# First and output products of the experts in one block, with bf16 gate products

## The chip, the cores and the metric

One core of one Trainium2 chip. TensorE multiplies matrices into PSUM, VectorE, ScalarE and GpSimd work on tiles in SBUF, and SyncE issues most of the DMA. The metric is the time of one execution in device microseconds (us); less is better.

## The reference

A decoder block on 1024 tokens of width 1024. The change lies in its last part, the product-key expert mixer. For each token eight heads choose 16 of 16384 experts each; every expert is a pair of vectors u and v. Cut to what matters:

```python
q = (xt @ wq).reshape(TOKEN_BLOCK, PEER_HEADS, 2, half)
s1 = jnp.einsum('thd,hkd->thk', q[:, :, 0], key1)
s2 = jnp.einsum('thd,hkd->thk', q[:, :, 1], key2)
v1, i1 = lax.top_k(s1, PEER_TOPK)
v2, i2 = lax.top_k(s2, PEER_TOPK)
...
sc, pos = lax.top_k(comb, PEER_TOPK)
...
gate = jax.nn.softmax(sc, axis=-1)
act = jax.nn.gelu(jnp.einsum('thkd,td->thk', u[experts], xt), approximate=False) * gate
return jnp.einsum('thk,thkd->td', act, v[experts])
```

After it come a residual, scaled by g2, and a final RMS norm.

## The kernel before

The kernel doesn't gather. It computes the hidden value of every expert for every token, multiplies it by a gate that is zero for experts not chosen, and multiplies the result by all of v. Each product of fp32 matrices is split: a = hi + lo, and three products (hi hi, hi lo, lo hi) in the fast fp32r format are added (`PARTS`). The two stages that the change touches come last, each a block of instruction streams that are written out by hand per engine and tied by semaphores.

**Stage `ph` (`stage_peer_topk`).** 136 tiles of weights pass through `tile` (L2121): 48 matmuls of 512 columns each. 8 tiles are the heads' query weights, 128 are u. Per tile SyncE loads `u_raw` (L2057), ScalarE makes the high part (`high`, L2175), VectorE the low part (`low`, L2254), ScalarE applies Gelu to the product (`take_hidden`, L2180) and SyncE stores it to DRAM (`hidden`, L2061). Two buffers of each alternate, so VectorE's low part for tile n + 2 is made after tile n has been taken. The stage has three parts:
- eight periods of `PERIOD` = 8 tiles, one per head. In each, VectorE does the top-k selection of one head between the splits (sixteen maxima and searches per round, pair sums, look-ups of 128x3200 elements),
- a bridge of 7 tiles, and transposes of the chosen expert numbers and shares,
- 64 gate steps of one tile and 16 tokens. For each token VectorE makes two operands: `row_hot`, one where the first half of the expert number matches (L2404), and `col_hot`, the share where the second half matches (L2408). Their fp32 product summed over the 128 picks (L2166) is the gate of all 16384 experts for that token. Four banks of four tokens alternate. ScalarE copies the banks out (L2245), and every fourth step SyncE stores 4 MB of gates (L2101).

All buffers of the stage are then given back and all engines meet at a barrier.

**Stage `px` (`stage_peer_mix`).** 32 turns of four groups of 128 experts. Per group SyncE loads v, the hidden values and the gates (L2469 to L2473, 0.5 MB each); VectorE multiplies hidden by gate (L2546), ScalarE makes high parts (L2522, L2524), VectorE low parts (L2548, L2550). A turn is 16 blocks of 12 matmuls of 512 columns (L2506) into 8 PSUM banks, and VectorE adds each block to an accumulator in SBUF (`held_tiles`, L2585). The operands of a turn are prepared during the turn before, at blocks 1, 5, 9 and 13. The accumulator is cleared first (L2554). In the last turn VectorE and ScalarE add the residual and normalise (L2563 to L2576), after a last load of g2, the norm weight and h.

## Time and profile before

| | |
|---|---|
| median of 3 runs | 5376.34 us (5373.24 to 5382.1) |
| profiled execution, its own time | 5366.34 us |
| its span | 5364.7 us |
| TensorE / VectorE / ScalarE / GpSimd busy | 94% / 53% / 29% / 5% |
| stage `ph` / stage `px`, first to last matmul | 2155.7 to 3901.3 / 3950.9 to 5346.6 us |
| mean DMA rate | 132 GB/s |

The busy share is an average over stages with different limits. Matmuls are pipelined: a matmul of 512 columns is shown as 389 ns long while the next starts after some 227 ns, so the price of one is read from starts, not from lengths. An fp32 product appears as two records.

### The profile page before, as it was taken

How to read it: one execution, taken by the hardware profiler on the slowest of the kernel's cores; microseconds unless marked ns; L12 is line 12 of the kernel's file. 1: busy time of each engine (PE TensorE's matmuls, PEld its weight loads, DVE VectorE, ACT ScalarE, POOL GpSimd, SP SyncE). 2: the span in 40 equal slices, each digit the busy share in tenths (PEclk: the TensorE clock that was granted, in tenths of full speed). 3: DMA queues.
4: the chain of work that ended last, by engine and by line, in shares of the span. 5: the costliest groups of instructions: out<-in, count | busy, mean ns of one | idle time of the engine just before them, and what ended most of it. 6: DMA issues, size and time to landing. Idle time of an engine off the chain costs nothing. (4 is left out here: it accounts for less than half of the span.)

```text
span 5364.7 us, 69919 instructions
## 1 busy us (share of the span) xinstructions
PE 5029.8 (94%) x25070; PEld 4136.0 (77%) x25070; DVE 2869.8 (53%) x6216; ACT 1572.6 (29%) x2427; POOL 254.4 (5%) x340
## 2 busy tenths in 40 slices
PE   5599979998997998999999999999969999999998
PEld 1388867776886777788888888888858888888887
DVE  6511027776566344466666455555545555555556
ACT  2211125565565332222222222222211111111111
POOL 1100000000333110000000000000000000000000
PEclk8798989999998999999999999999989999999999
DMA  7332123332554552222222243333365555555554
GB/s 292 114 118 89 65 84 122 127 126 102 189 184 144 181 165 75 89 85 91 87 91 95 110 161 140 137 153 144 129 175 142 145 147 142 144 148 142 143 147 132
DMA packets 479906, 710.29 MB, mean 132 GB/s; under 512 B 286432, under 2 KB 334960, under 8 KB 474472
## 3 DMA queue, kind: packets, MB, share of 16 engines
q1 hardware_dynamic: 451080, 598.51, 34.9%
q0 software_dynamic: 22880, 96.79, 5.3%
q10 hardware_dynamic: 5760, 12.59, 0.6%
q8 instruction: 107, 1.75, 0.1%
q14 instruction: 79, 0.65, 0.0%
HBM read 487.32 MB, written 220.49 MB: 132 GB/s over the span
## 5 line engine op out<-in xcount | busy, mean ns | idle before, releaser
L2121 PE MATMUL ph_hid_ps<-ph_n_hi,ph_u_hi 128*128 128x512 f32 x2176 | 855.0, 393 | 8.1 <-ACTq L2196 8.0
L2121 PE MATMUL ph_hid_ps<-ph_n_lo,ph_u_hi 128*128 128x512 f32 x2176 | 847.9, 390 | 0.0
L2121 PE MATMUL ph_hid_ps<-ph_n_hi,ph_u_lo 128*128 128x512 f32 x2176 | 847.8, 390 | 0.0
L2506 PE MATMUL px_out_ps<-px_v_hi,px_weight_hi 128*128 128x512 f32 x2048 | 798.0, 390 | 49.6 <-DVEq L2557 49.6
L2506 PE MATMUL px_out_ps<-px_v_lo,px_weight_hi 128*128 128x512 f32 x2048 | 797.7, 390 | 0.0
L2506 PE MATMUL px_out_ps<-px_v_hi,px_weight_lo 128*128 128x512 f32 x2048 | 797.6, 389 | 0.0
L2585 DVE TENSOR_TENSOR held_tiles<-held_tiles,px_out_ps 128x512 f32<-128x512 f32 x512 | 350.4, 685 | 594.2 <-PE px_out_ps L2506 594.2
L2254 DVE TENSOR_TENSOR ph_u_lo<-ph_u_raw,ph_u_hi 128x1024 fp32r<-128x1024 f32 x136 | 166.7, 1226 | 707.4 <-ACT ph_u_hi L2175 707.0
L2180 ACT ACTIVATE ph_hidden<-ph_hid_ps 128x1024 f32<-128x1024 f32 x128 | 131.2, 1025 | 1209.7 <-PE ph_hid_ps L2121 1209.7
L2506 PEld LDWEIGHTS px_out_ps<-px_v_hi,px_weight_hi 128*128 128x128 f32 x2048 | 385.0, 188 | 129.9 <-DVEq L2557 49.8
L2121 PEld LDWEIGHTS ph_hid_ps<-ph_n_hi,ph_u_hi 128*128 128x128 f32 x2176 | 409.4, 188 | 91.9 <-DVE ph_u_lo L2254 8.3
L2121 PEld LDWEIGHTS ph_hid_ps<-ph_n_hi,ph_u_lo 128*128 128x128 f32 x2176 | 409.0, 188 | 85.3
L2121 PEld LDWEIGHTS ph_hid_ps<-ph_n_lo,ph_u_hi 128*128 128x128 f32 x2176 | 409.4, 188 | 82.8
L2506 PEld LDWEIGHTS px_out_ps<-px_v_hi,px_weight_lo 128*128 128x128 f32 x2048 | 385.0, 188 | 80.2
L2506 PEld LDWEIGHTS px_out_ps<-px_v_lo,px_weight_hi 128*128 128x128 f32 x2048 | 385.1, 188 | 79.9
L2524 ACT ACTIVATE px_weight_hi<-px_raw 128x1024 fp32r<-128x1024 f32 x128 | 136.1, 1064 | 1040.9 <-DVE px_raw L2546 1040.9
L2408 DVE TENSOR_SCALAR held_tiles<-ph_iota,held_tiles 128x128 f32<-128x128 f32 x1024 | 284.3, 341 | 0.0
L2166 PEld LDWEIGHTS ph_gate_ps<-held_tiles,ph_row_hot 128*128 128x128 f32 x2048 | 238.4, 192 | 5.0
L859 PE MATMUL at_acc<-proj_n1T_hi,at_w_hi 128*128 128x512 f32 x512 | 213.8, 418 | 30.0 <-ACTq L1050 27.1
L2166 PE MATMUL ph_gate_ps<-held_tiles,ph_row_hot 128*128 128x128 f32 x2048 | 238.8, 275 | 0.0
L859 PE MATMUL at_acc<-proj_n1T_hi,at_w_lo 128*128 128x512 f32 x512 | 203.7, 398 | 0.0
L859 PE MATMUL at_acc<-proj_n1T_lo,at_w_hi 128*128 128x512 f32 x512 | 203.0, 396 | 0.0
(319 smaller groups left out, 7926.2 us busy)
## 6 DMA issues: line engine op xcount, KB each, us to landing
ph_u_raw<-in_tiles SPq DMA_DIRECT2D x136, 512.0 KB, 3.6
scratch_hidden<-ph_hidden SPq DMA_DIRECT2D x128, 512.0 KB, 2.6
scratch_gate_tiles<-ph_gates SPq DMA_DIRECT2D x16, 4096.0 KB, 12.8
px_v_raw<-in_v_experts SPq DMA_DIRECT2D x128, 512.0 KB, 3.5
px_raw<-scratch_hidden SPq DMA_DIRECT2D x128, 512.0 KB, 5.3
px_gate<-scratch_gate_tiles SPq DMA_DIRECT2D x128, 512.0 KB, 6.5
proj_w_ch<-in_w_ch SPq DMA_DIRECT2D x49, 512.0 KB, 3.7
mr_w<-in_ada_w POOLq DMA_DIRECT2D x6, 4096.0 KB, 19.6
```

The lines of the kernel that those rows point to most:

```text
L859: mm = pe.matmul(acc[c][:], w[p][a][:, k, :], n1T[b][:, k, c * HALF:(c + 1) * HALF], start=(k == 0 and a + b == 0), stop=(k == KD - 1 and ...
L2121: mm = pe.matmul(hid_ps[r][:, c * HALF:(c + 1) * HALF], u[r][a][:, k, :], n2[b][:, k, c * HALF:(c + 1) * HALF], start=(k == 0 and a + b == ...
L2166: mm = pe.matmul(gate_ps[b][:, t, :], row_hot[b][:, t, :], col_hot[b][:, t, :], start=True, stop=True)
L2180: act.activation(hidden[r][:], hid_ps[r][:], ACT.Gelu).then_inc(taken[r], 1)
L2254: dve.tensor_tensor(u[r][1][:], u_raw[r][:], u[r][0][:].bitcast(F32), ALU.subtract).then_inc(u_lo[r], 1)
L2408: ins = dve.tensor_scalar(col_hot[b][:, t, :], iota[:], chosenT[:, 1, tok], chosenT[:, 2, tok], ALU.is_equal, ALU.mult)
L2506: mm = pe.matmul(out_ps[b][:], weight[q][j][wp][:, t * P:(t + 1) * P], v[q][j][vp][:, c * HALF:(c + 1) * HALF], start=(j == 0 and wp + vp ...
L2524: act.activation(weight[q][j][0][:], raw[r][:], ACT.Copy).then_inc(weight_hi[r], 1)
L2585: dve.tensor_tensor(part, part, out_ps[b][:], ALU.add).then_inc(out_taken[b], 1)
```

## The change

- A period has six tiles in place of eight. The 16 tiles saved there (`TAIL`) run after the gate steps.
- The two stages are one block, with no barrier between. The `px` code stands in `stage_peer_topk`. Its buffers are those of the first products where they are free: the second set of operands in `n2`, the raw loads in `u_raw` and `hidden`, four of the eight PSUM banks in `hid_ps`, the other four in `gate_ps`.
- Experts 0 to 3 are loaded into slabs of `held` and prepared during the tail tiles `FIRST_AT` = 6, 8, 10, 12. Expert 4 and 5 are loaded after the last tile. Turn 0 copies its blocks into the accumulator in place of adding them to a cleared one. h arrives in eight loads at the end; g2 and the norm weight are loaded early.
- The gate operands are bf16. `row_hot` and `col_hot` are ones and zeros, and the share is split once into three bf16 terms. VectorE makes two products of `col_hot` with a term, ScalarE the third (L2376 of the new kernel), ahead of `take_hidden`. TensorE adds three products per token.
- The order of VectorE's pieces between the six splits of a period is another.

```diff
-PERIOD = 8
...
+PERIOD = 6
...
+GATE_TILE0 = 1 + PH * PERIOD + BRIDGE
+TAIL_TILE0 = GATE_TILE0 + S // 16
+TAIL = TILES_IN - TAIL_TILE0
...
-        row_hot = [sp.sb(f"row_hot{b}", [P, TOK, NK]) for b in range(NBANK)]
-        gates = [sp.sb(f"gates{s}", [P, NK, GATE_TOK]) for s in range(2)]
+        with ExitStack() as second:
+            def gates_sb(name, shape, dt=F32):
+                return second.enter_context(nc.sbuf_tensor(f"ph_{name}", shape, dt))
+
+            row_hot = [gates_sb(f"row_hot{b}", [P, TOK, NK], BF16) for b in range(NBANK)]
+            share = [gates_sb(f"share{n}", [P, S], BF16) for n in range(2)]
+            gates = [gates_sb(f"gates{s}", [P, NK, GATE_TOK]) for s in range(2)]
...
-        col_hot = [held[:, b // 2, (b % 2) * HALF:(b % 2 + 1) * HALF].rearrange("p (t n) -> p t n", t=TOK) for b in range(NBANK)]
...
+        weight0, v0 = ([[sp.sb(f"{name}0{j}_{p}", [P, S], F32R)[:] for p in ("hi", "lo")] for j in range(NJ)] for name in ("weight", "v"))
+        weight1, v1 = ([[of[:, 2 * j + p, :] for p in range(2)] for j in range(NJ)] for of in n2)
+        weight, v = (weight0, weight1), (v0, v1)
+        v_raw = [sp.sb(f"v_raw{r}", [P, D])[:] for r in range(2)]
...
+        acc = held
+        h_in = [weight0[t // 2][t % 2].bitcast(F32) for t in range(TT)]
+        norm_w = sp.sb("norm_w", [P, D])[:]
...
+            return held[:, slab, :].bitcast(BF16)[:, b * HALF:(b + 1) * HALF].rearrange("p (t n) -> p t n", t=TOK)
+
+        col_hot = [in_held(0, b) for b in range(NBANK)]
+        term = [[in_held(slab, b) for b in range(NBANK)] for slab in (1, 6, 7)]
...
+        FIRST_AT = (6, 8, 10, 12)
...
+                def load_expert(e, r, m, to):
+
                     if m is not None:
                         sync.wait_ge(v_lo[r], m)
...
+                for y in range(TAIL):
+                    n = TAIL_TILE0 + y
+                    store(n - PH, n % 2, n // 2)
+                    if n + 4 < TILES_IN:
+                        load(n + 4, n % 2, n // 2 + 2)
+                    if y == FIRST_AT[0] - 3:
+                        for b in range(NBANK):
+                            sync.wait_ge(gates_mm[b], S // PER_STEP + 1)
+                        for s in range(2):
+                            sync.wait_ge(gates_stored[s], 16 * (BLOCKS // 2 + 1))
+                        for j in range(2):
+                            sync.wait_ge(hid_stored[j], 16 * 3)
+                            load_expert(j, j, None, staged_first)
+                    if y == FIRST_AT[2] - 1:
+                        for j in range(2, NJ):
+                            load_expert(j, j % 2, 1, staged_first)
+                sync.wait_ge(hid_stored[0], 16 * (1 + 67))
+                sync.wait_ge(hid_stored[1], 16 * (1 + 61))
                 for r in range(2):
...
                 for r in range(2):
...
+                    sync.wait_ge(hid_mm[r], TILES_IN // 2)
+                for r in range(2):
+                    load_expert(NJ + r, r, 2, staged)
...
+                    for b in range(NBANK):
+                        pe.wait_ge(hot_ready[b], j + 1)
+                        pe.wait_ge(gates_taken[b], j + 1)
+                        pe.wait_ge(third_ready[b], j + 1)
+                        for t in range(TOK):
+                            for n in range(3):
+                                mm = pe.matmul(gate_ps[b][:, t, :], row_hot[b][:, t, :], term[n][b][:, t, :], start=(n == 0), stop=(n == 2))
...
+                gate_blocks(pe, step)
+                for n in range(TAIL_TILE0, TILES_IN):
+                    tile(n % 2, n // 2)
+
+                def turn(i2, q, first):
...
+                def turn(i2, q, first):
                     i = 2 * i2 + q
...
                         for b in range(NOUT):
                             t, c = divmod(b0 + b, 2)
-                            pe.wait_ge(out_taken[b], i * USES + (b0 // NOUT + 1))
+                            if first and b0 == 0 and b < NBANK:
+                                pe.wait_ge(gates_taken[b], S // PER_STEP + 1)
+                            elif first and b0 == 0:
+                                pe.wait_ge(taken[(b - NBANK) // 2], TILES_IN // 2 + 1)
+                            elif first:
+                                pe.wait_ge(out_taken[b], 1)
+                            else:
+                                pe.wait_ge(out_taken[b], i * USES + b0 // NOUT)
...
+                def step(k, s, x):
+                    j = 8 * k + (4 * s + x)
+                    r, m = x % 2, GATE_TILE0 // 2 + 4 * k + (4 * s + x) // 2
+                    for b in range(NBANK):
+                        act.wait_ge(col_ready[b], j + 1)
+                        for t in range(TOK):
+                            ins = act.activation(term[2][b][:, t, :], col_hot[b][:, t, :], ACT.Copy,
+                                                 scale=chosenT[:, 2, bass.ds(j * PER_STEP + (b * TOK + t), 1)])
+                        ins.then_inc(third_ready[b], 1)
+                    take_hidden(r, m, m - 1 if r == 0 else m - 7)
+                    high(r, m + 1)
+                    if x == 0:
+                        act.wait_ge(gates_stored[s], 16 * k + 16)
+                    for b in range(NBANK):
...
+                for y in range(TAIL):
+                    n = TAIL_TILE0 + y
+                    take_hidden(n % 2, n // 2, n // 2 - 1 if n % 2 == 0 else n // 2 - 7)
+                    if n + 2 < TILES_IN:
+                        high(n % 2, n // 2 + 1)
+                    if y in FIRST_AT:
+                        high_parts(0, 0, FIRST_AT.index(y), staged_first)
+                for j in range(NJ):
+                    high_parts(0, 1, j, staged)
...
+                dve.wait_ge(turned, 6)
+                own = Steps(dve, share_step)
+                for n in range(2):
+                    own.of(dve.tensor_copy(share[n][:], chosenT[:, 2, :]))
+                    own.wait()
+                    own.of(dve.tensor_tensor(chosenT[:, 2, :], chosenT[:, 2, :], share[n][:], ALU.subtract))
+                    own.wait()
+                for b in range(NBANK):
+                    dve.sem_inc(gates_mm[b], 1)
+
+                def step(k, s, x):
+                    j = 8 * k + (4 * s + x)
+                    for b in range(NBANK):
+                        dve.wait_ge(gates_mm[b], j + 1)
+                        dve.tensor_tensor(row_hot[b][:], iota[:].unsqueeze(1).to_broadcast([P, TOK, NK]),
+                                          chosenT[:, 0, bass.ds(j * PER_STEP + b * TOK, TOK)].unsqueeze(2).to_broadcast([P, TOK, NK]), ALU.is_equal)
+                        toks = bass.ds(j * PER_STEP + b * TOK, TOK)
+                        dve.tensor_tensor(col_hot[b], iota[:].unsqueeze(1).to_broadcast([P, TOK, NK]),
+                                          chosenT[:, 1, toks].unsqueeze(2).to_broadcast([P, TOK, NK]), ALU.is_equal).then_inc(col_ready[b], 1)
+                        dve.wait_ge(col_ready[b], j + 1)
+                        for n in range(2):
+                            ins = dve.tensor_tensor(term[n][b], col_hot[b], share[n][:, toks].unsqueeze(2).to_broadcast([P, TOK, NK]), ALU.mult)
+                        ins.then_inc(hot_ready[b], 1)
...
+                for y in range(TAIL):
+                    n = TAIL_TILE0 + y
+                    if n + 2 < TILES_IN:
+                        low(n % 2, n // 2 + 1)
+                    if y in FIRST_AT:
+                        prepare(0, 0, FIRST_AT.index(y), staged_first)
...
                         part = acc[:, t, c * HALF:(c + 1) * HALF]
-                        dve.tensor_tensor(part, part, out_ps[b][:], ALU.add).then_inc(out_taken[b], 1)
+                        if first:
+                            dve.tensor_copy(part, out_ps[b]).then_inc(out_taken[b], 1)
+                        else:
+                            dve.tensor_tensor(part, part, out_ps[b], ALU.add).then_inc(out_taken[b], 1)
                         if not last and n % NJ == 1:
```

What moves on the engines, at three places. VectorE, the last bank of a gate step. `held_tiles` is where `col_hot`, the terms and the shares lie; ISA and REGISTER_ALU are register arithmetic. Before:

```order
L2404 ISA
L2404 TENSOR_TENSOR ph_row_hot<-ph_iota,held_tiles 128x512
L2408 ISA
L2408 TENSOR_SCALAR held_tiles<-ph_iota,held_tiles 128x128
L2408 ISA
L2408 TENSOR_SCALAR held_tiles<-ph_iota,held_tiles 128x128
L2408 ISA
L2408 TENSOR_SCALAR held_tiles<-ph_iota,held_tiles 128x128
L2408 ISA
L2408 TENSOR_SCALAR held_tiles<-ph_iota,held_tiles 128x128
L2253 ISA
L2254 TENSOR_TENSOR ph_u_lo<-ph_u_raw,ph_u_hi 128x1024
```

After:

```order
L2579 ISA
L2579 TENSOR_TENSOR ph_row_hot<-ph_iota,held_tiles 128x512
L2582 ISA
L2582 TENSOR_TENSOR held_tiles<-ph_iota,held_tiles 128x512
L2586 ISA
L2586 TENSOR_TENSOR held_tiles<-held_tiles,ph_share 128x512
L2586 REGISTER_ALU
L2586 TENSOR_TENSOR held_tiles<-held_tiles,ph_share 128x512
L2423 REGISTER_ALU
L2424 TENSOR_TENSOR ph_u_lo<-ph_u_raw,ph_u_hi 128x1024
```

Four scaled comparisons of 128 columns have become one comparison of 512 and two products of 512.

ScalarE at the end of one step's operands and on to the gate copies. Before:

```order
L2179 ISA
L2180 ACTIVATE ph_hidden<-ph_hid_ps 128x1024
L2174 ISA
L2175 ACTIVATE ph_u_hi<-ph_u_raw 128x1024
L2242 ISA
L2244 ISA
L2245 ACTIVATE ph_gates<-ph_gate_ps 128x128x4 x4
```

After:

```order
L2376 ISA
L2376 ACTIVATE held_tiles<-held_tiles 128x128
L2313 ISA
L2314 ISA
L2315 ACTIVATE ph_hidden<-ph_hid_ps 128x1024
L2309 ISA
L2310 ACTIVATE ph_u_hi<-ph_u_raw 128x1024
L2382 ISA
L2384 REGISTER_ALU
L2385 ACTIVATE ph_gates<-ph_gate_ps 128x128x4 x4
```

The third terms (L2376, sixteen a step) now stand ahead of the copy of the hidden tile (L2315).

TensorE between the last tile and the first output product. Before:

```order
L2121 MATMUL ph_hid_ps<-ph_n_lo,ph_u_hi 128x512
L2121 MATMUL ph_hid_ps<-ph_n_hi,ph_u_lo 128x512
L2166 MATMUL ph_gate_ps<-held_tiles,ph_row_hot 128x128 x16
L2052 UNCONDITIONAL_BRANCH
L2492 UNCONDITIONAL_BRANCH
L2510 UNCONDITIONAL_BRANCH
L2510 ISA
L2506 MATMUL px_out_ps<-px_v_hi,px_weight_hi 128x512
```

After:

```order
L2223 MATMUL ph_hid_ps<-ph_n_hi,ph_u_hi 128x512
L2223 MATMUL ph_hid_ps<-ph_n_lo,ph_u_hi 128x512
L2223 MATMUL ph_hid_ps<-ph_n_hi,ph_u_lo 128x512
L2296 MATMUL ph_gate_ps<-ph_v_hi,ph_weight_hi 128x512
L2296 MATMUL ph_gate_ps<-ph_v_lo,ph_weight_hi 128x512
L2296 MATMUL ph_gate_ps<-ph_v_hi,ph_weight_lo 128x512
```

The gate product and the three branches between the blocks no longer stand there; the output product follows a tile.

## Rows read from the trace of the kernel before

**Rows 1.** The page: a group (busy, mean; idle before it), a DMA issue (us to landing).

```profile
L2506 PE MATMUL px_out_ps<-px_v_hi,px_weight_hi 128*128 128x512 f32 x2048 | 798.0, 390 | 49.6 <-DVEq L2557 49.6
...
scratch_hidden<-ph_hidden SPq DMA_DIRECT2D x128, 512.0 KB, 2.6
```

**Rows 2.** Busy time by stretch: PE, PEld, DVE, ACT, POOL (instructions), clock, DMA share, GB/s.

```profile
2601.00:2690.00 89.00, 89.00 (x395) 73.64 (x394) 58.99 (x243) 20.53 (x20) 0.00 (x0) 1.00 0.26 87
2990.00:3895.00 905.00, 905.00 (x4997) 786.83 (x4996) 484.91 (x1321) 249.50 (x372) 0.00 (x0) 1.00 0.36 140
3895.00:3955.00 60.00, 10.36 (x54) 8.83 (x54) 21.18 (x13) 12.37 (x14) 0.00 (x0) 0.59 0.78 236
```

**Rows 3.** Timeline of gate steps (start, us, engine): ScalarE, VectorE, then TensorE.

```profile
3015.39 1.02 ACT L2180 ACTIVATE ph_hidden<-ph_hid_ps 128x1024 f32<-128x1024 f32 x1 [10.39 <-PE ph_hid_ps L2121]
...
3017.39 1.23 DVE L2254 TENSOR_TENSOR ph_u_lo<-ph_u_raw,ph_u_hi 128x1024 fp32r<-128x1024 f32 x1 [6.72 <-ACT ph_u_hi L2175]
3018.53 0.69 DVE L2404 TENSOR_TENSOR ph_row_hot<-ph_iota,held_tiles 128x512 f32<-128x512 f32 x1
3019.13 1.11 DVE L2408 TENSOR_SCALAR held_tiles<-ph_iota,held_tiles 128x128 f32<-128x128 f32 x4
...
3883.09 3.73 PE L2166 MATMUL ph_gate_ps<-held_tiles,ph_row_hot 128*128 128x128 f32 x32
...
3897.56 3.73 PE L2166 MATMUL ph_gate_ps<-held_tiles,ph_row_hot 128*128 128x128 f32 x32
```

**Rows 4.** Timeline of TensorE: a bf16 pair in the attention, fp32 records in the scan.

```profile
1297.96 0.28 PE L876 MATMUL at_logit_ps<-at_causal_b,at_ident_b 128*128 128x128 bf16 x2
1298.08 0.61 PE L888 MATMUL at_turn_ps<-at_ident,at_diff 128*128 128x128 f32 x4
...
1499.77 0.61 PE L1404 MATMUL ssd_y_ps<-ssd_x_dt,ssd_weights 128*128 128x64 f32 x4
1500.21 0.65 PE L1407 MATMUL ssd_y_ps<-ssd_state,ssd_cT 128*128 128x256 f32 x2
```

**Rows 5.** Timeline between the expert stages: SyncE's queue, VectorE, TensorE.

```profile
3914.25 0.35 SPq L2469 DMA_DIRECT2D px_v_raw<-in_v_experts  x1
...
3943.93 6.88 DVE L2554 MEMSET held_tiles<- 128x8192 f32 x1 [1.66 <-issue]
...
3950.93 0.79 PE L2506 MATMUL px_out_ps<-px_v_hi,px_weight_hi 128*128 128x512 f32 x1 [49.64 <-DVEq L2557]
...
3956.64 0.47 PE L2506 MATMUL px_out_ps<-px_v_lo,px_weight_hi 128*128 128x512 f32 x1
```

**Rows 6.** Timeline, same stretch: the gate slice's issue, and what waited for the landings.

```profile
3919.93 0.43 SPq L2473 DMA_DIRECT2D px_gate<-scratch_gate_tiles  x1
...
3922.05 1.23 DVE L2546 TENSOR_TENSOR px_raw<-px_raw,px_gate 128x1024 f32<-128x1024 f32 x1 [31.26 <-DMA px_gate<-scratch_gate_tiles]
...
3927.02 1.23 DVE L2546 TENSOR_TENSOR px_raw<-px_raw,px_gate 128x1024 f32<-128x1024 f32 x1 [1.40 <-DMA px_gate<-scratch_gate_tiles]
```

**Rows 7.** Timeline of ScalarE in the scan.

```profile
1501.95 1.27 ACT L1574 ACTIVATE ssd_decay<-ssd_crow,ssd_cum 128x128 f32<-128x128 f32 x4
```

**Rows 8.** Chain of waits that ended last (start, us, what).

```profile
3950.93 1352.19 PE px_out_ps L2506 x5952
5304.53 15.46 DMA px_h<-scratch_h
```

**Rows 9.** Timeline of VectorE at the end.

```profile
5320.02 0.69 DVE L2563 TENSOR_SCALAR px_norm_w<-px_norm_w 128x1024 f32<-128x1024 f32 x1 [10.75 <-DMA px_h<-scratch_h]
5359.70 1.29 DVE L2576 SCALAR_TENSOR_TENSOR px_h<-px_h,px_rstd,px_norm_w 128x1024 f32<-128x1024 f32 x1
```

**Rows 10.** Timeline of VectorE in a head: searches, a look-up pass.

```profile
2549.56 0.09 DVE L2278 MATCH_VALUE_LOAD ph_index<-ph_top,ph_score 128x8 f32 x1
2553.54 0.29 DVE L2278 FIND_INDEX8 ph_index<-ph_top,ph_score 128x8 uint32<-128x128 f32 x1
...
2564.02 3.49 DVE L2314 TENSOR_TENSOR ph_hot<-ph_hot,ph_pair_id 128x3200 f32<-128x3200 f32 x1
```

318 lines of the change are left out of this document (141 added, 177 removed).

## The prediction

> **What bounds the kernel now.** I began with the page's list of costliest groups. TensorE's products of the two expert stages lead it. The only idle time of any size there is 49.6 us, ahead of the output products [rows 1]. The busy time per stretch comes next [rows 2]. In a head of the top-k selection (89 us, eight tiles) TensorE is busy throughout and VectorE for 59.0. In the gate stage TensorE is busy for all of 905 us and VectorE for 484.9. Between 3895 and 3955 TensorE has 10.4 us of work in 60, at a mean clock of 0.59. So TensorE's stream is the bound through both stages, and the one hole lies between them. In the timeline of two gate steps [rows 3] the gate products of a step start 14.47 us after those of the step before, as 32 records in 3.73 us.
>
> The units come from there. In the chain of waits 5952 output matmuls of 512 columns (31 of the 32 turns) take 1352.19 us [rows 8]. Without the 2.8 us of slow start found below that is 0.2267 us each. A tile of the first products has 48 of the same shape, 10.9 us, so the gate products hold TensorE for 14.47 - 10.9 = 3.57 us a step, and there are 64 steps.
>
> **The hole between the stages.** Before, the last gate copy is followed by the last store, a barrier and new buffers; the first load of the next stage is issued at 3914.25, VectorE clears the accumulator from 3943.93, and TensorE starts at 3950.93 after 49.64 us of waiting [rows 5]. It then runs at the lower of its two clocks (the stretch's mean is 0.59): the fourteenth matmul starts at 3956.64, 5.71 us after the first, where thirteen intervals of 0.2267 are 2.95. That is 2.8 us. After, 16 of the 136 tiles stand between the gate products and the output products. They are taken from the top-k selection, so they cost nothing new (16 x 10.9 = 174 us leave one place and enter the other). Beside them lie the loads and splits of experts 0 to 3. One expert's gate slice landed 7.1 us after its issue while another's transfers were under way [rows 6], and each preparation (after tile 6, 8, 10, 12 of these 16) has at least one tile of lead more than that. VectorE adds 3.6 us per preparation to 1.2 us in a 10.9 us tile. The clearing of the accumulator goes as well (turn 0 copies). So 49.6 + 2.8 = **52.4 us** go.
>
> What can be late next is turn 1. Its loads use the buffers of the last tiles. They are queued behind the last store of hidden values: about 1.3 us to the end of its copy, 2.6 to its landing [rows 1], 7.8 for expert 4 (3914.25 to 3922.05, [rows 5, 6]), so its parts are there some 12 to 13 us after TensorE's last tile; expert 5's come 5.0 us later (3922.05 to 3927.02). VectorE waits in that preparation from 5.5 us on, with the output copies behind it. TensorE needs the first of those banks at 10 x 2.72 = 27 us, and VectorE comes to it at about 17. Turn 1 wants its operands at 43.6 us, and the fourth preparation ends at about 42.5, bound by the fourteenth output block, as in every turn. Cost 0. If each landing were 10 us late, some 5 to 15 us.
>
> **The gate products.** Before, 32 fp32 records, 0.112 us apart. After, 48 bf16 passes of 128 columns. The trace has a pair of that shape in the attention [rows 4]: it starts at 1297.96 and what follows it starts at 1298.08, so 0.060 us each. By proportion to the 512-column matmul it is 0.2267 / 4 = 0.057. The floor is 128 columns at 2.4 GHz, 0.0533. The ceiling is the fp32 record of 64 columns in the scan: four from 1499.77 to the next instruction's start at 1500.21, 0.110 each, as much as one of 128 columns. I take 0.058, between the two nearest: 48 x 0.058 = 2.78, a step of 13.7 us, and 64 x (3.57 - 2.78) = **-51 us**. The ends are 64 x (2.56 - 3.57) = -65 and 64 x (5.28 - 3.57) = +109.
>
> **What stands beside it.** VectorE's 512-element comparison starts 0.60 us ahead of what follows it [rows 3]. After, a bank of operands is a comparison (0.60), a second one that it must wait out before reading it (0.69 + 0.02) and two products (0.60 each; no row shows the bf16 product, and I take the fp32 comparison of the same size): 2.53 us. Four banks and the split are 10.1 + 1.14 = 11.3 us of 13.7, so VectorE alone doesn't bind; before it was 484.9 / 905 of 14.47, or 7.8 [rows 2]. The new thing is a ring. The third terms stand on ScalarE ahead of the copy of the hidden tile. Behind that copy stands the split of the next tile, for which VectorE waits ahead of the next banks. Once round: three banks 7.6, to the end of the fourth's second comparison 1.3, four scaled copies of 128 columns 1.25 (the scan's four, with a tensor bias, took 1.27 [rows 7]), then from the start of the hidden copy to the start of the next bank 3018.53 - 3015.39 = 3.14 [rows 3]: 13.3 us. That is 0.4 less than TensorE's step. The ring is hidden, and just so. Its ends: with products at half their price it is 11.5; with 0.7 us for each VectorE operation and 1.7 for the scaled copies 14.6, 64 x 0.9 = +58 us.
>
> The split of the shares into three terms (two casts, two subtractions over 1024 columns, 4 us) delays the first banks only. The first step then waits for its fourth bank: **+2 us**, at most 5.
>
> **Six tiles per head.** TensorE's time per head is 89 us for eight tiles and the scores (89 - 87.2 = 1.8), and becomes 6 x 10.9 + 1.8 = 67.2 us. VectorE's is 59.0 less two splits of 1.15, 56.7. Its longest stretch between two splits is half a look-up (two passes of 3.5 us), some 1 us of small operations for the expert numbers and one round of sixteen searches (2549.56 to 2553.8, 4.3) [rows 10]: 12.3 + 1.15 against a tile of 10.9. It is 2.6 us late there, and TensorE wants that split 7 us later, since two tiles are in flight. The next stretch is 3.5 us and pays it back. Cost 0; if a head ran 3 us over, 8 x 3 = +24.
>
> **The end.** Of the residual and the norm, VectorE's chain sets the end: it starts when the last load lands at 5320.02 and runs to 5361 [rows 9], while TensorE is done 192 matmuls after 5303.1, at 5346.6. Before, 5 MB are loaded in 15.46 us from 5304.53 [rows 8]; after, the 1 MB of g2 and norm weight has been loaded long before. 4 MB at that rate are 12.4: **-3 us**, between 0 and -6.
>
> **Sum.** -52.4 - 51 + 2 - 3 = -104. The profiled execution took 5366.3 us, so 5262. The median of the runs shown lies 10 us above the profiled execution, which gives 5272.
>
> **Rivals.**
> 1. *The ring takes over.* It needs only 3% more than 13.3 us. For it: no row shows a bf16 product on VectorE or a tensor scale on ScalarE. Against: every price in it is one of a 1x fp32 operation. At 14.2 us a step it costs 32 us: 5304.
> 2. *The weight loads show.* Each pass has its own load, and the 512-column matmuls lie 0.2267 apart where 512 columns at 2.4 GHz are 0.2133, so 0.0133 us of each is not columns. If the same is added to 0.0533 a pass is 0.067, a step 14.1: +27 us, 5299. Against it is the pair at 0.060 [rows 4], but two in a row are not 48. The Trainium skill (TensorE: Matmul & The Clock Gate, "Back-to-back issue gap") has a rule that speaks more strongly against the change: in a sustained stream of loads and matmuls of 128 columns it gives about 81 ns each, because both operations set the spacing. By its figure a step would be 14.8 us, longer than today's, and the time 5342; no run here shows it yet, and the pair in the trace disagrees.
> 3. *The turn is late.* Landings behind the last store hold VectorE's queue and turn 1 starts without operands: +12 us, 5284. What speaks for it is that three transfers per expert stand behind one store. What speaks against is the 26 us of slack worked out above.
> 4. *Slower than before.* Passes keep the price of the fp32 record of 64 columns, 0.110: the scan shows that fewer columns did not make a pair cheaper. A step is then 16.2 us, and 5272 + 64 x 2.5 = 5432. It decides from where a step exceeds 14.47 + 52/64 = 15.3 us, that is from 0.092 us a pass.
> 5. *The head binds.* VectorE does not keep up with six tiles: +24, 5296.
>
> **How the numbers follow.** Forecast 0.54 (own range 5258 to 5287), ring 0.17, loads 0.12, turn 0.08, head 0.04, slower 0.05. All but the last lie over 1% below 5376, and a measurement of this kernel tells 0.2% (11 us). Of rival 4's 0.05 one part is a pass near 0.092, within 0.2%, and so is a little of the others: faster 0.94, same 0.02, slower 0.04. The low end is the forecast with 0.0533 a pass and the full gain at the end: 5272 - 14 - 3 = 5255, and less some spread of runs 5252. The high end takes in the ring at 14.2 and the loads: 5312.
>
> **What would show it.** In the profile after: no idle time on TensorE ahead of the output products, and clock 1.0 across the junction; 64 gate steps at about 13.7 us; gate passes 0.058 apart (0.067 or more is rival 2, over 0.09 rival 4); idle time of TensorE in a gate step with a third term or an operand bank as its releaser would be the ring; such idle time in the heads, released by the split, rival 5; one stall some 44 us after the last tile, rival 3. The last load should land some 3 us sooner after TensorE's turn 30. The prediction is wrong if TensorE still waits tens of microseconds anywhere, or if a step is over 14.4 us.

## The result, and the profile after

| | before | after | ratio (95% interval) |
|---|---|---|---|
| median | 5374.79 us (5371.1 to 5382.1, 4 runs) | 5340.07 us (5334.87 to 5351.04, 4 runs) | 0.9936 (0.9924 to 0.9948) |
| profiled execution, its span | 5364.7 us | 5349.4 us | |

The forecast was 5272 us, in a range from 5252 to 5312. The kernel became faster by 35 us where 104 were forecast, so the forecast was 68 us too low.

The profiled execution is the slowest of the four, and nine microseconds of its distance arose before the changed stage: the first tile starts at 2164.57, before it was 2155.77. In the profiles of this study that start lies between 2155.8 and 2171.9 us and follows nothing that was changed, so stages are compared from there. From the first tile to the end of the span it was 5364.7 - 2155.8 = 3208.9 us before, and is 5349.4 - 2164.6 = 3184.8: 24 us less.

Most of what was forecast is there, and beside it a cost that was not. Across the junction, in the timeline of TensorE, where [rows 5] had 49.64 us of waiting (start, us, engine, line, operation):

```profile
3941.59 0.39 PE L2223 MATMUL ph_hid_ps<-ph_n_hi,ph_u_lo 128*128 128x512 f32 x1
3941.82 0.39 PE L2296 MATMUL ph_gate_ps<-ph_v_hi,ph_weight_hi 128*128 128x512 f32 x1
```

The first output product follows the last tile product by 0.23 us, one interval. Two gate steps in the same timeline, as in [rows 3]:

```profile
3027.67 2.85 PE L2270 MATMUL ph_gate_ps<-held_tiles,ph_row_hot 128*128 128x128 bf16 x48
...
3041.35 2.85 PE L2270 MATMUL ph_gate_ps<-held_tiles,ph_row_hot 128*128 128x128 bf16 x48
3048.46 0.77 PE L2223 MATMUL ph_hid_ps<-ph_n_hi,ph_u_hi 128*128 128x512 f32 x1 [4.26 <-issue]
3049.03 0.63 PE L2223 MATMUL ph_hid_ps<-ph_n_lo,ph_u_hi 128*128 128x512 f32 x1
...
3051.16 0.50 PE L2223 MATMUL ph_hid_ps<-ph_n_hi,ph_u_hi 128*128 128x512 f32 x1
3054.83 0.58 PE L2223 MATMUL ph_hid_ps<-ph_n_lo,ph_u_hi 128*128 128x512 f32 x1 [3.17 <-issue]
```

They lie 13.68 us apart; forecast 13.7. What nobody forecast stands behind the second: TensorE waits 4.26 us, does seven matmuls 0.43 us apart (the granted clock is the lower one, 1.2 GHz, from 3048.0 to 3051.4; 0.2267 us is the rate at 2.4), and waits 3.17 us again. The releaser is "issue": nothing that the profile shows. The longest totals in the list of TensorE's waits in the two stages (who, released by: us, times, longest):

```profile
PE ph_hid_ps L2223 <- issue: 53.4, 14, 4.4
PE ph_hid_ps L2223 <- DVE ph_u_lo L2424: 7.8, 1, 7.8
```

Fourteen waits on issue are two at each of seven places (2923, 3044, 3164 and so on), and these are the seven back edges of TensorE's gate loop of eight steps, the jumps from the end of a round to its start. Between the second gate step (2838.06) and the 64th (3764.9, the last tile step before sixteen tiles of 10.88 us that end at 3941.8) lie 926.9 us. 62 steps of 13.67 are 847.5. The other 79 us are the seven edges, 11.3 us each: 7.6 of waiting, the rest the lower clock. The busy times of the stretch, with those of [rows 2] to compare (PE, PEld, DVE, ACT, POOL, clock, DMA share, GB/s):

```profile
2820.00:3770.00 950.00, 894.64 (x6116) 752.58 (x6116) 714.06 (x1082) 571.66 (x1404) 0.00 (x0) 0.96 0.37 138
```

TensorE is no longer busy throughout, and its mean clock is 0.96. The branch at the end of the round shows where the time goes. These are the rows of TensorE's queue for the loop's line, in the kernel before (L2044) and after (L2106): how long the branch took in ns (least, median, most), and its first and last start in us:

```profile
L2044 PEldq COMPARE_BRANCH  x7: 76/208/231, 3089.1 to 3783.5; - x7
L2106 PEldq COMPARE_BRANCH  x8: 83/4958/4997, 2922.6 to 3766.8; - x8
```

The shortest is the last, which isn't taken. A branch back took 0.2 us before and 4.7 to 5.0 us after. The transfers of instructions tell why. In 210 us of the gate stage, 3060 to 3270 (queue and kind: packets, MB, share of 16 engines):

```profile
q8 instruction: 14, 0.23, 0.4%
q14 instruction: 7, 0.06, 0.1%
```

A packet on q8 is 16 KB. In the kernel before, q8 moved nothing between 3110 and 3290, but ran at one piece in 20 to 30 us where the code is straight: a loop that is held isn't transferred again. Here it moves nine pieces per round. The trace has 1334 instructions of TensorE in a gate round before and 1590 after: matmuls, a weight load for each, waits and register arithmetic, an fp32 product counting as two matmuls. The transfers count the same way. In straight code one piece goes for 256 such instructions (256.7 on average in e2 below, 256.1 in e4, where fp32 products counted once would give 206). So the round grew from 5.2 pieces to 6.2. (The recorded expectations count 1038, 1550, 1584 and 2060: these leave waits out and take an fp32 product once. The trace has 1334, 1590, 1633 and some 2666.)

The Trainium skill (Runtime: NRT & Kernel Launch, "Instruction fetch mechanics") says that instructions come in 16 KiB blocks of 256, that TensorE has 128 KiB for them, that they are fetched ahead purely in sequence, and that a taken branch whose target lies outside the current window of two pages forces a fetch before execution goes on. The packets agree with the blocks. The window of two doesn't agree: rounds of 5.2 pieces came back without a transfer. What decides for a loop was put to experiments.

### The profile page after: what moved, and what is told of

Same layout as the page of the kernel before. It is cut to its first block, busy times and chain, and to the rows that moved or that the text cites. A ratio compares the mean times of both kernels' runs of the same rounds, so it can differ in the third digit from the quotient of the medians.

```text
span 5349.4 us, 73631 instructions
## 1 busy us (share of the span) xinstructions
PE 5004.9 (94%) x26094; PEld 4090.6 (76%) x26094; DVE 3090.3 (58%) x5963; ACT 1888.0 (35%) x3451; POOL 254.3 (5%) x340
## 4 chain that ended last, share of the span: by engine, by line
PE 57%; issue 1%; DVE 1%; DMA 0%; ACT 0%; SPq 0%; DVEq 0%
PE ph_hid_ps L2223 28%; PE ph_gate_ps L2296 13%; PE ph_hid_ps L2296 13%; PE ph_gate_ps L2270 3%; PE ph_score_ps L2232 1%; DVE held_tiles L2618 0%; DVE held_tiles L2620 0%; DMA ph_weight_lo<-scratch_h 0%; DVE held_tiles L2626 0%; DVE held_tiles L2638 0%; DMA ph_u_raw<-in_tiles 0%; DVE held_tiles L2586 0%; SPq L2207 0%; DVE held_tiles L2582 0%; DVE held_tiles L2570 0%
## 5 line engine op out<-in xcount | busy, mean ns | idle before, releaser
L2376 ACT ACTIVATE held_tiles<-held_tiles 128x128 bf16<-128x128 bf16 x1024 | 328.4, 391 | 308.6 <-DVE held_tiles L2582 305.4
L2296 PE MATMUL ph_gate_ps<-ph_n_lo,ph_n_hi 128*128 128x512 f32 x1536 | 353.4, 389 | 0.0
L2296 PE MATMUL ph_hid_ps<-ph_n_lo,ph_n_hi 128*128 128x512 f32 x1536 | 353.4, 389 | 0.0
L2586 DVE TENSOR_TENSOR held_tiles<-held_tiles,ph_share 128x512 bf16<-128x512 bf16 x512 | 331.4, 689 | 37.5 <-DVE held_tiles L2582 2.3
L2315 ACT ACTIVATE ph_hidden<-ph_hid_ps 128x1024 f32<-128x1024 f32 x128 | 130.7, 1021 | 610.9 <-PE ph_hid_ps L2223 610.9
L2638 DVE TENSOR_TENSOR held_tiles<-held_tiles,ph_gate_ps 128x512 f32<-128x512 f32 x248 | 169.9, 686 | 287.7 <-PE ph_gate_ps L2296 287.7
L2296 PEld LDWEIGHTS ph_gate_ps<-ph_n_lo,ph_n_hi 128*128 128x128 f32 x1536 | 288.4, 188 | 59.8
L2296 PEld LDWEIGHTS ph_hid_ps<-ph_n_lo,ph_n_hi 128*128 128x128 f32 x1536 | 288.4, 188 | 59.8
L2638 DVE TENSOR_TENSOR held_tiles<-held_tiles,ph_hid_ps 128x512 f32<-128x512 f32 x248 | 169.8, 686 | 283.6 <-PE ph_hid_ps L2296 283.6
L2398 ACT ACTIVATE ph_n_hi<-ph_u_raw 128x1024 fp32r<-128x1024 f32 x64 | 68.1, 1064 | 513.0 <-DVE ph_u_raw L2596 513.0
L2296 PE MATMUL ph_gate_ps<-ph_v_lo,ph_weight_hi 128*128 128x512 f32 x512 | 199.3, 389 | 0.0
```

Source lines behind the costliest of these rows:

```text
L2296: mm = pe.matmul(out_ps[b], weight[q][j][wp][:, t * P:(t + 1) * P], v[q][j][vp][:, c * HALF:(c + 1) * HALF], start=(j == 0 and wp + vp == ...
L2315: act.activation(hidden[r][:], hid_ps[r][:], ACT.Gelu).then_inc(taken[r], 1)
L2376: ins = act.activation(term[2][b][:, t, :], col_hot[b][:, t, :], ACT.Copy, scale=chosenT[:, 2, bass.ds(j * PER_STEP + (b * TOK + t), 1)])
L2398: act.activation(weight[q][j][0], of[1][r], ACT.Copy).then_inc(weight_hi[r], 1)
L2586: ins = dve.tensor_tensor(term[n][b], col_hot[b], share[n][:, toks].unsqueeze(2).to_broadcast([P, TOK, NK]), ALU.mult)
L2638: dve.tensor_tensor(part, part, out_ps[b], ALU.add).then_inc(out_taken[b], 1)
```

## Experiments

e8 and e10 leave lower terms of the share out of the gates, and e9 makes the gates in fp32; the others leave the arithmetic as it is. In the table, waits are TensorE's on issue within the two stages (of e14's six one, of 0.2 us, lies at the first tile).

| | change on TensorE | edges | waits on issue | median us (range) | ratio to before (95%) |
|---|---|---|---|---|---|
| e1 | 4 steps a round | 15 | none | 5269.8 (5265.2 to 5278.1) | 0.9806 (0.9790 to 0.9823) |
| e2 | 64 steps written out | 0 | none | 5268.3 (5266.6 to 5276.1) | 0.9810 (0.9790 to 0.9829) |
| e3 | edge behind a tile | 7 | none | 5269.7 (5262.6 to 5274.2) | 0.9804 (0.9784 to 0.9824) |
| e4 | kernel before, 16 steps | 2 | 15.1 us in 4 | 5392.2 (5384.4 to 5403.9) | 1.0041 (1.0028 to 1.0055) |
| e5 | 1 step peeled | 6 | none | 5270.8 (5266.3 to 5277.2) | 0.9804 (0.9788 to 0.9821) |
| e6 | 16 steps | 3 | 22.9 us in 6 | 5302.9 (5301.3 to 5307.0) | 0.9866 (0.9849 to 0.9882) |
| e7 | 16 steps, edge behind a tile | 3 | 9.5 us in 3 | 5287.6 (5278.2 to 5290.9) | 0.9840 (0.9824 to 0.9857) |
| e8 | e1, one pass for three | 15 | 3.4 us in 15 | 5273.6 (5264.8 to 5274.6) | 0.9813 (0.9797 to 0.9829) |
| e9 | overlap alone, fp32 gates | 7 | none | 5318.9 (5311.1 to 5326.6) | 0.9905 (0.9890 to 0.9921) |
| e10 | e1, two terms | 15 | none | 5221.6 (5213.4 to 5227.0) | 0.9716 (0.9702 to 0.9729) |
| e11 | 16 steps, edge in mid-tile | 3 | none | 5272.2 (5271.8 to 5273.7) | 0.9813 (0.9798 to 0.9828) |
| e12 | 4 steps peeled | 6 | none | 5272.6 (5266.9 to 5279.0) | 0.9809 (0.9787 to 0.9831) |
| e13 | after, 20 idle instructions | 7 | none | 5271.0 (5262.1 to 5276.3) | 0.9806 (0.9787 to 0.9825) |
| e14 | e5, 40 idle instructions | 6 | 22.5 us in 6 | 5300.9 (5295.6 to 5307.9) | 0.9867 (0.9849 to 0.9885) |

From the first tile to the end of the span, the profiled executions of e1, e2, e3, e5, e12 and e13 took 3105.5 to 3106.4 us, and that of after 3184.8: 79 us, the seven edges.

**Is it the loop's length?** e1 shortens the round (its edit, cut to TensorE's loop), e2 takes the loop away:

```diff
-                gate_blocks(pe, step)
+                with pe.Fori(0, S // 16 // 4) as k:
+                    for x in range(4):
+                        step(k, x)
```

> The kernel after, with TensorE's gate loop of four steps in sixteen rounds in place of eight steps in eight (773 instructions a round for 1550); the other engines' loops are unchanged. In the profile after, each of the seven back edges of that loop costs 11.3 us over the 13.67 us of a step (7.4 us in two waits on issue, the rest at the lower clock), 79 us in all. Theory A, the body no longer stays with the engine and is fetched anew in each round: the waits vanish and the time is 5340 - 79 = 5261 us (5252 to 5270). Theory B, every back edge behind short passes costs that, whatever the body's length: fifteen edges, 5340 + 90 = 5430 us. Theory C, the 4 MB gate stores or something else at the end of every second group of four steps holds TensorE, and the loop has nothing to do with it: 5340 us.

> The kernel after, with TensorE's 64 gate steps written out, so that there is no back edge between them at all. Theory A: 16 KB pieces are fetched in sequence ahead of their use, no waits, 5261 us (5252 to 5275); if fetching in sequence could not keep up with passes of 0.057 us, waits of a few us spread over the steps would show. Theory B: 5261 us too, since no edge is left. Theory C: 5340 us.

Both land on theory A, e1 at the upper end of its range. It has more edges than after and no wait; the one change takes off 70 us by the medians, and what is left is within 3 us of the forecast. The 4 MB gate stores (theory C) stand as before. The stretch of e1, and its instruction transfers from 3060 to 3270, to set beside those above:

```profile
2820.00:3770.00 950.00, 947.67 (x6464) 800.64 (x6464) 726.37 (x1095) 582.97 (x1420) 0.00 (x0) 1.00 0.40 152
```

```profile
q14 instruction: 10, 0.08, 0.1%
q8 instruction: 1, 0.02, 0.0%
```

q14 goes on and q8 doesn't, and only TensorE's loop was changed: q8 is TensorE's. In e2 q8 runs at three or four pieces in 60 us through the whole stage, and TensorE never waits: fetching in sequence keeps up with passes of 0.057 us. Only the jump back is dear.

**Does it matter what stands at the edge?** e3 turns the loop by half a step (its edit, cut); e4 gives the kernel before a round of sixteen steps.

```diff
...
+                tile(0, GATE_TILE0 // 2)
                 gate_blocks(pe, step)       # step: gates of j, then tile of j + 1
-                for n in range(TAIL_TILE0, TILES_IN):
+                for n in range(TAIL_TILE0 + 1, TILES_IN):
```

> The kernel after, with TensorE's gate loop turned by half a step: the same 1550 instructions in a round, the same order of the work, but the back edge stands behind a tile's 512-column matmuls (0.227 us each) and not behind 48 gate passes (0.057 us each). Theory A1, the fetch is needed at each edge either way, but what has been issued ahead of the edge covers it when it lasts long enough (the head loop before, 1584 instructions, had no wait): no waits, 5261 us (5252 to 5275). Theory A2, the fetch itself takes longer than anything issued ahead: the waits stay, 5340 us. Theory B (an edge behind short passes costs): 5261 us. Theory C: 5340 us.

> The kernel before, with TensorE's gate loop of sixteen steps (three rounds and a written-out rest) in place of eight: about 2060 instructions a round for 1038, fp32 passes (0.112 us apart) as before. Theory A: the body is fetched anew in each round, and at the two back edges TensorE waits, less than the 7.4 us of after since the passes last twice as long: 5375 + 2 x (3 to 8) = 5381 to 5391 us, with waits on issue at two places in the profile. Theories B and C: no change, 5375 us, no such waits.

e3 gave the time of theory A1, but not for its reason: the stage has no q8 transfers after the first round, with a round as long as in after. So it says nothing of whether long matmuls ahead of the edge cover a fetch, and opened the question of place below. e4 is slower by 0.4%, 23 us for two edges where 6 to 16 were expected. The fp32 passes last twice as long and yet the waits are no shorter than in after, 7.6 us an edge (the TensorE timeline at the edges):

```profile
3214.50 0.77 PE L2121 MATMUL ph_hid_ps<-ph_n_hi,ph_u_hi 128*128 128x512 f32 x1 [2.53 <-issue]
3218.88 0.59 PE L2121 MATMUL ph_hid_ps<-ph_n_hi,ph_u_lo 128*128 128x512 f32 x1 [3.19 <-issue]
3455.73 0.47 PE L2121 MATMUL ph_hid_ps<-ph_n_hi,ph_u_hi 128*128 128x512 f32 x1 [2.97 <-issue]
3462.85 0.59 PE L2121 MATMUL ph_hid_ps<-ph_n_hi,ph_u_lo 128*128 128x512 f32 x1 [6.42 <-issue]
```

e6, e7 and e11 have rounds that can't stay (about 3180 instructions, 12 pieces), and differ only in what stands at the edge (edit cut):

```diff
-                gate_blocks(pe, step)
+                tile(0, GATE_TILE0 // 2)                              # e7; e11: with halves=(0,); not in e6
+                with pe.Fori(0, 4) as k:
+                    tile(0, GATE_TILE0 // 2 + 8 * k, halves=(1,))     # e11 alone
+                    for x in range(16):
+                        step(k, x)    # e6: tile, gates; e7: gates, next tile; e11: as e7, of x == 15 halves=(0,)
```

> The kernel after, with TensorE's gate loop of sixteen steps in four rounds: 3100 instructions a round, which no theory lets stay, and three back edges behind 48 gate passes each. Each edge costs what those of after do, 11.3 us: 5269 + 34 = 5303 us, with six waits on issue in the profile, some 4 and 3 us each.

> The kernel of e6 turned by half a step: 3100 instructions a round and three back edges, each behind a tile's 512-column matmuls. Theory A1, the engine's queue ahead of the edge lasts as long as the fetch when it holds 512-column matmuls (the head loop before had its transfers at the edges some microseconds ahead of them, and no wait): 5269 us, no waits on issue, though the transfers are there. Theory A2, nothing covers them: as e6, 5303 us. The two runs differ in nothing else.

> The kernel of e6 and e7 (3100 instructions a round, three back edges) with the edge in the middle of a tile: 24 matmuls of 512 columns ahead of it and 24 behind. With passes ahead of the edge and a tile behind (e6) it cost 34 us, with a tile ahead and passes behind (e7) 18 us. The head loop of the kernel before has tiles on both sides, its transfers, and no wait. Theory A1: long matmuls on both sides cover both pieces, no waits, 5269 us. Theory A2: what stands beside the edge doesn't decide: 5287 to 5303 us.

e6 was forecast at 5303 and measured 5302.9: 11 us an edge. e7 lies between its two theories, at half of that; e11 takes it away, though it has q8 transfers throughout (three to five in 60 us). The waits of e7, then of e11, whose list has none on issue:

```profile
PE ph_gate_ps L2269 <- issue: 9.5, 3, 3.5
PE ph_hid_ps L2223 <- DVE ph_u_lo L2427: 7.9, 1, 7.9
```

```profile
PE ph_hid_ps L2224 <- DVE ph_u_lo L2431: 7.9, 1, 7.9
PE mo_turn_ps L1838 <- DVE mo_n L1924: 6.0, 1, 6.0
PE ph_gate_ps L2271 <- DVE held_tiles L2593: 3.0, 2, 1.8
```

So 24 long matmuls on both sides cover the jump, as in the head loop of before, whose round of 1633 instructions was fetched anew each time (q8 packets at 2437, 2442, 2445 and 2450 around an edge at 2444.7) with no wait in the list. The branch rows of that loop, of e7 and of e11 show how:

```profile
L2037 PEldq COMPARE_BRANCH  x3: 83/3723/3955, 2440.4 to 2803.0; - x3
L2274 PEldq COMPARE_BRANCH  x4: 83/6864/7266, 3031.4 to 3702.2; - x4
L2276 PEldq COMPARE_BRANCH  x4: 83/3628/3882, 3035.6 to 3692.2; - x4
```

The branch starts while matmuls handed over earlier still run: 4.1 us of long ones in e7 (3031.4 to 3035.5), but only 1.1 us of short passes in after (3043.15 to 3044.2). Where the branch takes 3.4 to 4.0 us, in the head loop and in e11, the long ones last about as long. In e7 it takes 6.7 to 7.3 us, and the wait of 3.2 us behind it is about what they don't cover. Why it takes longer there isn't settled by these runs.

**Why did a round of the same length stay in e3?** e5 and e12 write out steps ahead of the loop; e13 and e14 only add instructions that do nothing behind the first tile (edits cut).

```diff
-                gate_blocks(pe, step)
+                gate_step(0, GATE_TILE0 // 2, 0)                     # e12: four
+                with pe.Fori(0, 7) as k:
+                    for x in range(1, 9):                             # e12: 4 to 11
+                        gate_step(8 * k + x, GATE_TILE0 // 2 + 4 * k + x // 2, x % 2)
+                for x in range(57, 64):                               # e12: 60 to 63
+                    gate_step(x, (GATE_TILE0 + x) // 2, x % 2)
```

```diff
                 tile(0, 0, True)
+                for _ in range(40):                    # e13: 20 instructions of two waits; e14: 80 waits, on e5
+                    pe.wait_ge(u_lo[0], 1)
```

> The kernel after, with one gate step of TensorE written out ahead of the loop, seven rounds of eight steps, and seven steps written out behind it: the loop has the same 1550 instructions a round and its back edge stands behind the same 48 gate passes, but it begins 194 instructions later in TensorE's stream. The turned loop (e3, its start moved by some 100 instructions) had no transfer of instructions within its rounds, so it showed nothing of cover behind the edge. Theory P, it is the place of the loop's start against the 16 KB pieces that decides whether a body of this length stays: no 16 KB instruction transfers in the rounds, no waits, 5269 us (5260 to 5280). Theory Q, the length alone, or the edge behind short passes: six edges at 11.3 us, 5269 + 68 = 5337 us.

> The kernel after, with four gate steps of TensorE written out ahead of the loop, seven rounds of eight steps, and four steps written out behind it. The loop of 1550 instructions begins 768 instructions later than in after, three times 256, so it lies against 16 KB pieces (256 instructions of 64 bytes) as in after; in e3 (96 later) and e5 (192 later) it does not, and there it stayed. Theory P, the place against the pieces decides: it is fetched anew in each round, at the six back edges TensorE waits as in after, and the time is 5270 + 6 x 10 to 11.3 = 5330 to 5338 us. Theory P', steps written out ahead of the loop keep it resident for another reason: no transfers in the rounds, no waits, 5270 us.

> The kernel after with twenty more instructions on TensorE behind its first tile, each a wait that has long been met; nothing else is changed, and the gate loop of eight steps has its 1590 instructions (waits now counted) and its edge behind short passes. Its start moves by 20 instructions to the place against the 256-instruction pieces that e12's loop had. Theory P (1590 instructions touch seven pieces or eight, by the place of the start, and only seven can stay): no transfers in the rounds, no waits on issue, 5340 - 70 = 5270 us. Theory P' (written-out steps ahead of the loop are what helps): 5340 us.

> The kernel of e5 (one step written out ahead, seven rounds of eight; no transfers in the rounds, 5270.8 us) with forty more met waits on TensorE behind its first tile. That moves the loop's start from 201 to 241 (mod 256, on the scale where after's is 4, e12's 24 and e3's 101), by which it touches eight pieces wherever the border lies that these four runs leave possible. Theory P: transfers in every round, twelve waits on issue at six edges, 5271 + 60 to 68 = 5331 to 5339 us. Theory P': 5271 us.

e5 stayed, by theory P. e12 was to be fetched anew by P and wasn't. Its expectation rested on a count that left TensorE's wait instructions out; with them its loop lies 20 further on than after's, not at the same place. e13 tested that alone: after with twenty idle instructions more is faster than after by 69 us (5271.0 for 5340.1), with no wait on issue. Its branch is as short as that of before:

```profile
L2106 PEldq COMPARE_BRANCH  x8: 83/215/218, 2922.8 to 3688.1; - x8
```

That shows that the place of the loop decides here. Where the borders of the pieces lie is worked out from these runs and not seen. The trace of after agrees with a border just there: its second wait comes behind the seventh matmul of the round, some 15 instructions in, which is where a second piece would begin if the loop starts that far ahead of a border; 20 more put the start behind it. 1590 instructions are 6.2 pieces, and touch seven or eight; the six runs with this round fit, but for one edge of e14, if seven stay and eight don't. e14 pushed a loop that stayed back over the border, and it was fetched again, though only at five of the six edges (between 3030 and 3155 q8 moved nothing), and with one wait of 4.3 to 4.7 us at each, at 3159.96 for instance:

```profile
3159.96 0.47 PE L2223 MATMUL ph_hid_ps<-ph_n_hi,ph_u_hi 128*128 128x512 f32 x1 [4.43 <-issue]
```

Its cost was 30 us, 6 an edge, where 60 to 68 were expected: the direction of P, half the size. By the border inferred above this loop starts some 35 instructions ahead of one, so that the second piece has more time to arrive; that is argued, no run tests it. That a round of eight pieces can also stay for once was expected by no theory; it stays open.

**What are the parts worth?** e9 takes the bf16 part out of after (TensorE's side of the edit).

```diff
-                            for n in range(3):
-                                mm = pe.matmul(gate_ps[b][:, t, :], row_hot[b][:, t, :], term[n][b][:, t, :], start=(n == 0), stop=(n == 2))
+                            mm = pe.matmul(gate_ps[b][:, t, :], row_hot[b][:, t, :], col_hot[b][:, t, :], start=True, stop=True)
```

> The kernel after with the gate operands and products as they were before (fp32, one product per token, the share in the comparison, no third term on ScalarE): the overlapped turn and the six tiles per head alone. TensorE's round of eight gate steps is then as long as before's and should stay with the engine. By the prediction's terms -52.4 for the hole and -3 for the end: 5372 - 55 = 5317 us (5308 to 5325). If the overlap had a price of its own that e1 hides (a late turn, contention in the gate stage), the time is higher, and the bf16 part is worth more than the 51 us forecast; e1 less this run is that part, forecast 51 - 2 = 49 us.

The overlap alone is worth 5370.2 - 5318.9 = 51 us (forecast 55), and the bf16 part, with a loop that stays, 5318.9 - 5269.8 = 49 (forecast 49). From the first tile to the end of the span the two are 56 and 48 us (3208.9, 3153.2 and, in e1, 3105.7).

**How much slack had the ring?** e8 gives TensorE one pass in place of three and leaves all operands; e10 leaves out the third term, on ScalarE too (edits cut; both have e1's loop).

```diff
-                            for n in range(3):            # e8: term[0] alone
+                            for n in range(2):            # e10
...
-                    for b in range(NBANK):                # e10: ScalarE's third terms
-                        act.wait_ge(col_ready[b], j + 1)
```

> The kernel of e1 with one gate pass per token in place of three on TensorE (the products with the second and third term of the share are left out; VectorE and ScalarE make all operands as before). TensorE then needs 10.88 + 16 x 0.057 = 11.8 us a step, and the ring of the other engines sets the step if it is longer. By the prediction's sum the ring is 13.3 us: 64 x (13.3 - 13.67) = -24, 5246 us, with TensorE waiting for operands in every step. If the ring has as much slack as its lower bound (11.5): step 11.8, 5269 - 120 = 5149 us.

> The kernel of e1 without the third term of the share: ScalarE makes none and TensorE has two passes per token (this leaves the lowest bits of the gates out). TensorE's step falls to 10.88 + 32 x 0.057 = 12.7 us. With one pass per token and all operands kept (e8) the step was 13.68 us, which is the ring of VectorE and ScalarE through the third terms. Theory R, the ring goes with the third term, and VectorE alone needs 4 x 2.64 + 1.14 = 11.7 us: TensorE binds, 5269 - 64 x 0.91 = 5211 us. Theory S, it was VectorE's queue as a whole that set 13.68: 5269 us again.

e8 gains nothing, where at least 24 us were expected: TensorE has 11.8 us of work and its fourth bank comes every 13.68 us (2846.43 to 3489.29 in 47 steps). One turn of the ring in its timeline, VectorE, then ScalarE:

```profile
3244.97 1.23 DVE L2425 TENSOR_TENSOR ph_u_lo<-ph_u_raw,ph_u_hi 128x1024 fp32r<-128x1024 f32 x1 [1.86 <-ACT ph_u_hi L2311]
3246.11 0.69 DVE L2580 TENSOR_TENSOR ph_row_hot<-ph_iota,held_tiles 128x512 bf16<-128x512 f32 x1
3246.71 0.69 DVE L2583 TENSOR_TENSOR held_tiles<-ph_iota,held_tiles 128x512 bf16<-128x512 f32 x1
3247.54 1.29 DVE L2587 TENSOR_TENSOR held_tiles<-held_tiles,ph_share 128x512 bf16<-128x512 bf16 x2
3248.75 0.68 DVE L2580 TENSOR_TENSOR ph_row_hot<-ph_iota,held_tiles 128x512 bf16<-128x512 f32 x1
...
3254.03 0.68 DVE L2580 TENSOR_TENSOR ph_row_hot<-ph_iota,held_tiles 128x512 bf16<-128x512 f32 x1
...
3258.72 1.23 DVE L2425 TENSOR_TENSOR ph_u_lo<-ph_u_raw,ph_u_hi 128x1024 fp32r<-128x1024 f32 x1 [1.97 <-ACT ph_u_hi L2311]
```

```profile
3255.45 1.28 ACT L2377 ACTIVATE held_tiles<-held_tiles 128x128 bf16<-128x128 bf16 x4 [1.36 <-DVE held_tiles L2583]
3256.72 1.02 ACT L2316 ACTIVATE ph_hidden<-ph_hid_ps 128x1024 f32<-128x1024 f32 x1
3257.64 1.05 ACT L2311 ACTIVATE ph_u_hi<-ph_u_raw 128x1024 fp32r<-128x1024 f32 x1
```

A bank is 2.64 us (3246.11 to 3248.75). From one split to the next: 1.14 + 3 x 2.64 + 1.42 to the third terms, 1.27 for them, 0.92 and 1.08 to the next split, 13.75 here. e10 confirms what closes it: without the third term the gate products come every 12.78 us, and the time falls by 48 us, where 58 were expected. The pace explains part of that: every fourth or so step is 12.97, so the mean is 12.83 and 64 x 0.84 = 54. From the first tile to the end it is 52 us less than e1 (3053.4 for 3105.7).

```profile
2846.43 1.96 PE L2269 MATMUL ph_gate_ps<-held_tiles,ph_row_hot 128*128 128x128 bf16 x32
2859.21 1.98 PE L2269 MATMUL ph_gate_ps<-held_tiles,ph_row_hot 128*128 128x128 bf16 x32
2871.99 1.98 PE L2269 MATMUL ph_gate_ps<-held_tiles,ph_row_hot 128*128 128x128 bf16 x32
2884.94 1.96 PE L2269 MATMUL ph_gate_ps<-held_tiles,ph_row_hot 128*128 128x128 bf16 x32
```

With all three terms nothing was faster than e1, e2, e3, e5 and e13, which can't be told apart (1.9% under before, 1.3% under after). e10, with two terms, is 2.8% under before.

## Why the prediction was wrong, step by step

**The step that failed** is the one for the gate products, "64 x (3.57 - 2.78) = -51 us". It multiplied one step's price by 64, as if the steps were followed by nothing but one another. The price was right (a step 13.67, a pass (13.67 - 10.88) / 48 = 0.058), the count of steps was right, and a term was missing: three bf16 passes for one fp32 product lengthen TensorE's round from 1334 instructions to 1590, the round, where it lies in this kernel, no longer stays with the engine, and seven back edges cost 79 us in the profiled execution, 70 by the medians (5340.1 - 5269.8). The prediction itself put 48 passes where 32 fp32 records stood, and no step asked what that does to the loop. None of the rivals held it. Rival 3 and rival 5 priced waits at other places, and the first condition for being wrong ("if TensorE still waits tens of microseconds anywhere") came true for a reason that was not among the cases, so the range was too narrow by a whole kind of cost.

With a loop that stays (e1), from the first tile to the end it is 5276.4 - 2170.7 = 3105.7 us for 3208.9 before: -103, forecast -104. The other steps one by one:

- **The hole, -52.4.** Right: no idle time and a clock of 1.00 from 3942 to 3986. e9 gives it and the end together as 51 by the medians and 56 from the first tile on, forecast 55.
- **Turn 1.** Right. The parts of expert 4 were there 11.7 us after TensorE's last tile (forecast 12 to 13), those of expert 5 by 17.6 (forecast 17 to 18), VectorE waited 5.4 us, and TensorE not at all. Rival 3 didn't occur. The "26 us of slack" it was weighed against isn't worked out in the prediction; it is the way from expert 5's landing to turn 1 (43.6 - 17.6). The preparation as a whole had 1 us: its last part ended 42.5 us after the last tile, as forecast. VectorE's rows of the first two loads:

```profile
3953.52 1.22 DVE L2596 TENSOR_TENSOR ph_u_raw<-ph_u_raw,ph_hidden 128x1024 f32<-128x1024 f32 x1 [5.38 <-DMA ph_hidden<-scratch_gate_tiles]
3959.41 1.22 DVE L2596 TENSOR_TENSOR ph_u_raw<-ph_u_raw,ph_hidden 128x1024 f32<-128x1024 f32 x1
```

- **Weight loads (rival 2).** Didn't occur: 0.058 a pass in a row of 48, and no sign of the 81 ns that the Trainium skill (TensorE: Matmul & The Clock Gate, "Back-to-back issue gap") gives for a sustained stream of 128 columns. Rival 4 fell with it.
- **The ring.** The mechanism was right, its size 0.4 us short: 13.7 for 13.3. A bank is 2.64 for 2.53, since the second comparison's reader starts 0.83 us behind its start (forecast 0.71), and the fourth bank's part is 1.42 for 1.3. "Hidden, and just so" held by luck: the 0.4 us of slack weren't there. Ring (13.68 in e8) and TensorE's step (13.67) are the same length. The ends of 11.5 and 14.6 held it.
- **The first step, +2.** Right: one wait of 1.8 us for an operand bank.
- **Six tiles per head, 0.** Right: no waits, a head every 68.75 us for 90.7 before, the difference is two tiles. The forecast had 67.2: it took the 89 us of the window in [rows 2] for a head's period, and so had 1.8 for the scores where 90.7 gives 3.6.
- **The end, -3.** Right: TensorE ended 18.1 us ahead of the end of the span before; after, its last 43 matmuls are a row of 9.91 us from 5324.71, so it ends 14.8 us ahead.

## What to carry to other kernels

When an edit puts more instructions into a loop, count the engine's instructions in one round, weight loads and waits too, and set them against what the engine was seen to hold: look in the trace whether instruction packets go on after the first round, and how long the loop's branch takes. On TensorE here rounds of 1242 (the head loop after) and 1334 stayed, one of 1590 cost 70 us or nothing by its place, and one of 3180 came anew at every edge. Halve the round on that engine alone (the other engines' loops needn't change), or put the back edge into the middle of long matmuls. A step's price times the number of steps isn't a loop's price.

## What the runs showed of the hardware that was not expected

- A branch back took TensorE's queue 0.2 us when the round was held and 3.4 to 7.3 us when it wasn't.
- A back edge to instructions no longer held costs TensorE 11 us behind short passes in after and e6: two waits of 3 to 4 us each, and some 4 us by the lower clock after them (at 3048 seven matmuls about 0.43 us apart between the waits, eight more behind the second). In e14 there was one wait, and the edge cost 6 us.
- Twenty instructions that do nothing made a kernel 1.3% faster (e13 against after), through the place of a later loop alone. A comparison of two kernels can carry such a difference with no part of it in the edited code.
- Fetching in sequence was never late: e2 ran 64 written-out steps without a wait.
- VectorE's product of bf16 operands, 128x512 with the share broadcast, starts 0.60 us ahead of its follower, the same as the fp32 comparison: the narrower type gained nothing there.
